# Rider products of two weight rows at a time in the expert passes of a hybrid encoder step

## The reference

```python
def _moe(h, w_router, b_router, we1, we3, we2):
    x = h.reshape(B * T, D)
    logits = (x @ w_router).astype(f32) + b_router.astype(f32)
    top_v, top_i = lax.top_k(logits, TOP_K)
    gates = jax.nn.softmax(top_v, axis=-1)
    comb = jnp.sum(jax.nn.one_hot(top_i, N_EXPERTS, dtype=f32) * gates[..., None], axis=1)
    y = jnp.zeros(x.shape, f32)
    for e in range(N_EXPERTS):
        y = y + comb[:, e:e + 1] * _swiglu(x, we1[e], we3[e], we2[e]).astype(f32)
```

## Time and profile before

| | |
|---|---|
| median of 3 runs | 2233.93 us (2231.75 to 2235.88) |
| the profiled execution | 2235.12 us |
| its span, first to last instruction | 2233.4 us |
| TensorE busy | 2063.2 us (92%) |
| VectorE busy | 1308.9 us (59%) |
| ScalarE busy | 996.8 us (45%) |
| mean granted TensorE clock | 0.935 of full speed |
| bytes moved by DMA | 418.23 MB, mean 187 GB/s |

### The profile page before, as it was taken

One profiled execution on the slowest core, in us unless ns is written; L12 is line 12 of the kernel. 1 busy time (PEld: TensorE's weight loads), 2 busy tenths in 40 slices (PEclk: granted clock), 3 DMA queues, 4 the chain that ended last, 5 costly groups with the idle time before them and its releaser, 6 DMA issues.

```text
span 2233.4 us, 36658 instructions
## 1 busy us (share of the span) xinstructions
PE 2063.2 (92%) x14266; PEld 1708.0 (76%) x14292; DVE 1308.9 (59%) x2052; ACT 996.8 (45%) x1456; POOL 181.5 (8%) x271
## 2 busy tenths in 40 slices
PE   6999878898999999998998788979899999999996
PEld 4999745588999999998997445966566657788883
DVE  2657654354544545456477553555565657789884
ACT  5522125444423443435211264435444556677772
POOL 3000120110000000000000111111010010000201
PEclk7999769999999999999997699978999999999998
DMA  9222668533545454642223357126677788899994
GB/s 328 65 76 76 162 189 292 183 122 95 167 126 165 136 157 132 172 126 78 61 73 85 89 190 239 47 93 236 202 262 233 242 271 311 327 372 373 375 382 179
DMA packets 272094, 418.23 MB, mean 187 GB/s; under 512 B 21214, under 2 KB 216312, under 8 KB 271952
## 3 DMA queue, kind: packets, MB, share of 16 engines
q1 hardware_dynamic: 249984, 349.50, 47.1%
q0 software_dynamic: 21968, 66.72, 9.2%
HBM read 385.73 MB, written 29.59 MB: 186 GB/s over the span
## 4 chain that ended last, share of the span: by engine, by line
PE 84%; DVE 5%; ACT 4%; DMA 3%; issue 2%; POOL 0%; ACTq 0%; PEldq 0%; DVEq 0%; PEld 0%; POOLq 0%; SPq 0%
PE banks L941 80%; PE banks L945 4%; DVE scratch L2522 1%; ACT scratch L1887 1%; DMA weight_ring<-in_w_ada 1%; DVE region L2522 1%; ACT hidden_t L1887 1%; ACT region_split L1887 1%; DMA scratch<-bias_rows 1%; ACT region L1887 0%; DVE weights_lower L2522 0%; DMA hidden_t<-h_rows,pass_tokens 0%; ACTq L1902 0%; DMA region<-in_pool_scale 0%; DMA expert_ring<-in_we 0%
## 5 line engine op out<-in xcount | busy, mean ns | idle before, releaser
L941 PE MATMUL banks<-upper_parts,region_split 128*128 128x320 f32 x1664 | 390.2, 310 | 4.5 <-DVE upper_parts L2522 4.5
L941 PE MATMUL banks<-upper_parts,weights_lower 128*128 128x320 f32 (+1 forms) x1248 | 387.1, 310 | 0.0
L2522 DVE TENSOR_TENSOR expert_lower<-expert_ring,region_split 128x1408 fp32r<-128x1408 f32 (+1 forms) x198 | 286.1, 1469 | 103.7 <-PE banks L941 78.3
L941 PE MATMUL banks<-region_split 128*128 128x320 f32 (+1 forms) x1264 | 342.1, 333 | 3.0 <-DVE upper_parts L2522 3.0
L941 PEld LDWEIGHTS banks<-upper_parts,region_split 128*128 128x128 f32 x1664 | 284.5, 189 | 4.8 <-issue 4.8
L1887 ACT ACTIVATE region_split<-expert_ring 128x1408 fp32r<-128x1408 f32 (+1 forms) x198 | 241.6, 1256 | 57.8 <-DMA expert_ring<-in_we 45.4
L941 PEld LDWEIGHTS banks<-region_split 128*128 128x128 f32 x1264 | 223.0, 188 | 25.0 <-issue 8.4
L941 PEld LDWEIGHTS banks<-upper_parts,weights_lower 128*128 128x128 f32 (+1 forms) x1248 | 235.3, 189 | 0.0
L941 PE MATMUL banks<-region_split,upper_parts 128*128 128x384 f32 x732 | 234.3, 385 | 0.0
L2522 DVE TENSOR_TENSOR weights_lower<-weight_ring,region_split 128x2048 fp32r<-128x2048 f32 (+2 forms) x72 | 168.9, 2350 | 96.2 <-ACT region_split L1887 96.2
L1887 ACT ACTIVATE region_split<-weight_ring 128x2048 fp32r<-128x2048 f32 (+2 forms) x72 | 140.6, 1958 | 164.2 <-PE banks L941 162.5
(11 more groups left out here) (333 smaller groups left out, 3276.1 us busy)
## 6 DMA issues: line engine op xcount, KB each, us to landing
expert_ring<-in_we SPq DMA_DIRECT2D x176, 704.0 KB, 6.3
expert_ring<-in_we SPq DMA_DIRECT2D x121, 512.0 KB, 4.3
weight_ring<-in_w_ada SPq DMA_DIRECT2D x48, 1024.0 KB, 9.3
weight_ring<-in_w SPq DMA_DIRECT2D x88, 512.0 KB, 4.8
weight_ring<-in_w_in SPq DMA_DIRECT2D x24, 1024.0 KB, 5.3
weight_ring<-in_w SPq DMA_DIRECT2D x16, 1408.0 KB, 6.2
weight_ring<-in_w_out SPq DMA_DIRECT2D x8, 1024.0 KB, 6.9
y_rows<-residual_t POOLq DMA_DIRECT2D x4, 1760.0 KB, 23.6
```

The lines of the kernel that those rows point to most:

```text
L941: return nc.tensor.matmul(out, lhsT, rhs, start=first, stop=last)
L2522: return v.tensor_tensor(out, x, y, op)
```

## The change

In `up` and `down` the ride behind each row's products becomes a pair of rides behind every other row's: in `up` behind the odd rows c (rows c + 5 and c + 6), in `down` behind the even rows f (f + 5 and f + 6). The two groups of rides ahead of the first `up`s have six rides where they had five. What each ride computes, the ring, the other engines' programs and the number of rides stay.

```diff
@@ up
                             release[0] = True
-                            if ridden and c + LOOK < UP_ROWS:
-                                ride(place - 1 + LOOK, up_row=c + LOOK)
-                            if following and c + LOOK >= UP_ROWS:
-                                ride(place - 1 + LOOK, down_row=c + LOOK - UP_ROWS)
+                            for ahead in range(c + LOOK, c + LOOK + 2) if c % 2 else ():
+                                if ridden and ahead < UP_ROWS:
+                                    ride(place - 1 + ahead - c, up_row=ahead)
+                                if following and UP_ROWS <= ahead < UP_ROWS + LOOK:
+                                    ride(place - 1 + ahead - c, down_row=ahead - UP_ROWS)
                             if c == 13:
                                 turn_rows(0, 0)
@@ down
                             release[0] = True
-                            if ridden and f + LOOK < NF:
-                                ride(place - 1 + LOOK, down_row=f + LOOK)
-                            if rows == "ridden" and f + LOOK >= NF:
-                                ride(place - 1 + LOOK, up_row=f + LOOK - NF)
+                            for ahead in range(f + LOOK, f + LOOK + 2) if f % 2 == 0 else ():
+                                if ridden and ahead < NF:
+                                    ride(place - 1 + ahead - f, down_row=ahead)
+                                if rows == "ridden" and ahead >= NF:
+                                    ride(place - 1 + ahead - f, up_row=ahead - NF)
                             if rows and f == 0:
@@ before the first two up
                     turn_riders(5)
-                    for c in range(LOOK):
+                    for c in range(LOOK + 1):
                         ride(c, up_row=c)
                     up(True, False)
                     turn_rows(1, 1)
                     turn_riders(3)
-                    for c in range(LOOK):
+                    for c in range(LOOK + 1):
                         ride(place + c, up_row=c)
```

## The result

The changed kernel took 2216.77 us (median of 6 runs, 2212.78 to 2223.65), the kernel before 2233.56 us beside it (6 runs, 2231.06 to 2235.88). The ratio is 0.9927, with a 95% interval of 0.9912 to 0.9942: 16.8 us less, which is more than the 0.2% that the prediction gave as what a measurement can tell. The forecast was 2214.0 in a range of 2210 to 2223.

What follows compares the result with a forecast made beforehand. TensorE, busy 92% of the span, was taken to bound the kernel. Savings of 14.3 + 5.0 + 1.3 + 0.6 = 21.2 us less 1.4 us of waits gave 19.8 off the 2233.93 us median: 2214 us, range 2210 to 2223.

Steps and rivals of the forecast that it cites:

- The switch: In `up` and `down`, 61 switches from products to rides and back go: 0.357 us behind up rows, 0.334 behind down rows.
- The turns at f = 9 and f = 1: In `down`, where a turn follows the ride: 0.22 us saved a switch, six switches, 1.3 us in all.
- The starting groups: Ahead of the first `up`s: second group's sixth ride hides in idle time, 0.64 us saved; first group's counts 0, at worst 0.64 more.
- The waits for landings: TensorE waits for weight rows ridden a step earlier: 0.4 us per loop trip (0 to 1.5), 0.2 behind the loop; 1.4 together.
- TensorE idle before rides with the ring as its releaser: Sign of being wrong: TensorE waiting before rides for expert ring rows would point to rivals A or C.
- The distance allowed: From a row's release to its ride as second of a pair: 8.1 us in `up`, 6.5 us in `down`.
- the need: Time from a row's release to its landing: 6.45 us for row 12, 6.75 us with the trip's slowest landing.
- one wait of 0.2 us: In the pass after the loop, row 17 has 0.1 us to spare before its ride; 0.2 us counted, from 0 to 1.
- nothing queued on VectorE or ScalarE waits longer: `claim`s, `lower`s and copies see each ride at the same step or earlier, so their queues gain no waiting.
- A: Rival: the gain is there but half is lost to landings in ridden passes, about 2225 us; chance 0.15.
- B: Rival: the cost comes with each ride, not the switch, so time stays within 0.2% of 2234 us; chance 0.05.
- C: Rival: slower, second rides wait for rows landing 8.5 us after release in `up`, 6.9 in `down`; about 2252 us; chance 0.03.

Runs made afterwards that it cites:

- late_pairs: Changed kernel with each pair asked a step later (first ride later, second at its old step), starting groups of five: 2215.32 us, ratio 0.9904 to the kernel before.
- double_apart: Kernel before with each ride's products done twice, the first half inside the row's products with a switch of its own: 2347.69 us.
- start_of_five: Changed kernel with five rides in the second starting group, the sixth again alone behind the first up row: 2220.50 us, one run.
- pairs_down_only: Kernel before with pairs of rides in `down` only; `up` and starting groups as before: 2227.12 us, one run.
- pairs_up_only: Changed kernel with single rides again in `down`, pairs in `up` and starting groups of six kept: 2222.85 us, ratio 0.9938 to the kernel before.
- pairs_again: The changed kernel run once more without edit: 2219.99 us against 2236.93 for the kernel before, ratio 0.9921.
- double_together: Kernel before with each ride's products done twice, back to back, no switch added: 2309.23 us, one run.
- triples: Changed kernel with groups of three rides behind every third row: 2213.93 us; with VectorE's token rows also moved ahead of row 18's lower part, 2205.50 us.

## Why the prediction was right, and where its sum was off

**The switch (20.6 of the 21.2 us).** Right in its price. 5.46 and 3.98 us for two rows with a pair, 69.90 us for a trip of late_pairs without waits where 69.8 to 70.0 was expected, and double_apart confirm a price that was only a difference of three rows. The first section fits too, -2.23 us for 6 switches (2.14), though 0.24 us of it is a cheaper sixth ride (below).

**The turns at f = 9 and f = 1.** Counted at 0.22 us a switch. By the rule that the prediction took from the Trainium skill (TensorEngine Tiling (Array Packing), Key Properties) the one at f = 9 would be worth 0.33. From the last product of the row to the first behind the turn the kernel before takes 1.41 us (1732.12 to 1733.53) with a ride of 0.643 in between, so 0.77 without it, and the changed one 0.48 (1719.39 to 1719.87). That is 0.29 us saved: nearer to the rule. At f = 1 the same reading gives 2.78 us before (1711.57 to 1714.35), 2.35 without its ride of 0.429, and 2.22 with the change (1698.93 to 1701.15): 0.13 us saved, less than was counted. Together the two come to 0.42 us a trip for the 0.44 in the sum, so the total was right by two errors that cancel.

**The starting groups.** The 0.64 us for the sixth ride of the second group stands (start_of_five). That of the first group lengthened the time to the first product by 0.40 us, from 6.07 to 6.47, less than a ride at the full clock, so the bound of 0.64 more was not drawn on. That time differs from one execution to the next, though: 5.75 to 6.07 us with five rides over the profiles of kernels that do each ride once, and 6.07 to 6.47 with six.

**The waits for landings: the term that was mis-sized.** Counted at 0.4 us a trip with an end at 1.5, and 0.2 once behind the loop. The trips gave back 0.9, 1.2 and 1.6 us (70.60, 70.92, 71.30 less 69.7), 3.6 us for the 1.2 counted. TensorE idle before rides with the ring as its releaser was one of the prediction's own signs of being wrong, and it is there. The place was right, row 12 at f = 6 of `down`; in the third trip row 11, whose ride keeps its step, was late as well (0.42 us), which the prediction had not priced. The distance allowed (6.5 us) was right as well; the need was not 6.45 us. Here are the first product of f = 4, which releases row 12's place, the two rides at f = 6, the second of them late, and the loads of rows 11 and 12, all in the changed kernel (issue, then issue to landing):

```profile
1705.23 0.39 PE L941 MATMUL banks<-region_split 128*128 128x512 f32 x1
...
1711.06 0.85 PE L941 MATMUL banks<-expert_ring,mix_t 128*32 128x384 f32 x8
1712.59 0.85 PE L941 MATMUL banks<-expert_ring,mix_t 128*32 128x384 f32 x8 [0.67 <-DMA expert_ring<-in_we]
...
L671 SPq DMA_DIRECT2D expert_ring<-in_we x1: 333/333/333, 1704.6 to 1704.6; - x1
DMA to landing us min/median/max: 6.2/6.2/6.2
...
L671 SPq DMA_DIRECT2D expert_ring<-in_we x1: 333/333/333, 1705.8 to 1705.8; - x1
DMA to landing us min/median/max: 6.8/6.8/6.8
```

Row 12 was released at 1705.23 and landed 7.4 us later, at 1712.6, where the earlier trace rows had made it 6.45. Before, the rows 11 and 12 were asked for 2.1 us apart; now they are 1.2 us apart, because two rows behind a pair of rides follow each other without a ride in between. In the three trips row 12 took 5.2, 5.8 and 5.2 us from issue to landing before, and 6.6, 6.8 and 7.2 with the change. The two half changes say where that comes from: 6.6 to 6.9 us in pairs_down_only, which has the close question and the old pace of `up`, and 5.2 to 5.8 in pairs_up_only, which has the faster `up` and the old spacing in `down`. The DMA engines are no fuller: over twelve microseconds around these loads their share is 0.85 before (from 1715) and 0.83 with the change (from 1703), and the same two gathers of GpSimd for the next pass land in that stretch in both. The issues are 1.2 us apart and the landings 1.8, so some 0.6 us is row 12 behind row 11. Row 11 itself took 6.0 to 6.7 us for 5.1 to 5.9. How the two loads share the engines was not tried, and that part stays argued. The prediction did say that "rows come closer together", but for the speed of the whole trip, and took the landing time from loads that were evenly spaced. A change that bunches the consumer bunches the releases too. The spacing should have been worked out like the distance was.

**What was not in the sum.** In the passes behind the loop one wait of 0.2 us had been counted. There were 0.49, 0.53 and 0.33 us for rows (the middle one is the row 17 that the prediction had named), and one of a kind that was not foreseen, 0.55 us for ScalarE. TensorE's timeline shows the wait, and ScalarE's two lines ahead of it the cause:

```profile
1859.65 0.50 PE L941 MATMUL banks<-z_weights_upper,upper_parts 128*128 128x512 f32 x1 [0.55 <-ACT hidden_t L1889]
...
1857.35 1.38 ACT L1889 ACTIVATE region_split<-expert_ring 128x1408 fp32r<-128x1408 f32 x1 [1.36 <-DMA expert_ring<-in_we]
...
1859.01 1.08 ACT L1889 ACTIVATE hidden_t<-banks 128x512 f32<-128x512 f32 x2
```

The rows came late for ScalarE as well. It stood 1.36 us for one, where the kernel before has 0.28 us at the same row, and its copies out of the banks, which TensorE's `claim` waits for, were queued behind it. The prediction said that nothing queued on VectorE or ScalarE waits longer, since no ride comes later; it had left out the landings themselves.

**The clock behind the second starting group** is where I put the 0.7 us of the second section. Two windows of the changed kernel, inside the six rides and over the first products:

```profile
1570.00:1571.00 1.00, 1.00 (x12) 0.38 (x8) 0.98 (x1) 0.00 (x0) 0.69 (x2) 0.50 0.78 327
...
1581.00:1582.00 1.00, 1.00 (x5) 1.00 (x4) 0.57 (x2) 0.96 (x2) 0.00 (x0) 0.50 0.07 16
```

In the kernel before the clock fell only in the idle time ahead of the first products and was back up with the first of them (0.91 from 1588 to 1589). In the changed kernel it fell to the 1.2 GHz level during the rides, rose, and fell again within the transposes and over the first row's products; these products took some 3.1 us for 2.1. The same section lost 0.9 to 1.0 us to its sum in pairs_again, late_pairs and start_of_five. It is not shown that the change brings this about. In pairs_down_only this section has the code of the kernel before, its clock stayed low until 1585.4 with products from 1582.2 on, and it took 56.82 us for 55.34. So the kernel before in its one profile may have been lucky by up to 1.5 us, and the 6.6 us given back are uncertain by as much. No kernel tested the clock by itself.

**The rivals.** A (half the gain lost, 2225) had the right mechanism at a third of its size: the trips gave back 3.6 us where it needed 12. B fell by double_together. C (slower) needed landings of 6.9 us after release in `down`, and 7.4 was reached for row 12. But its price was for three pairs of each `down` and seven of each `up`, and in the trips of `up` no ride waited. The condition came true for one row of a trip, and not at ten places.

**The total.** In the stretch 14.6 us for the 19.8 forecast; by the runs 16.8 us for 19.9 (2216.77 for 2214), the difference between two medians that each have their spread. The time lies inside the narrower 2211 to 2219 as well. The mechanism was right, and the term for the landings was a third of what it should have been; that the clock, ScalarE and the waits behind the loop added only some 3 us more is luck, for the sum had only 0.2 us for them.

**Left open.** The end of the expert stage, behind four plain passes, is the same code in all kernels, and took from 37.05 to 39.10 us (37.75 before, 37.05 in the changed kernel). What sets it wasn't tried, so the last line of the table is no gain of the change.

## What to carry to other kernels

Where small column-tiled products stand between full ones, read the price of going there and back from three rows (with, without, and in a run of their own), and group as many as the data's arrival allows: pairs gave 0.7 to 0.8% here, the late ones 1.0%, triples 1.4% once VectorE's order was mended. Group by delaying the first, not by asking earlier for the last: late_pairs had pairs with one wait left of seven. When a consumer is bunched, work out the new spacing of the releases and of the loads, and look down the in-order queues of the other engines for work that is ready but stands behind a bunched wait.

## What was not expected of the hardware

- A ride behind a ride costs its columns alone, 15.17 us for 27 rides where the columns say 15.0, while each switch there and back costs 0.31 to 0.36 us with 384 columns a tile, and 0.33 us with 256.
- TensorE's clock can fall while the engine is busy throughout. In double_apart it fell to the 1.2 GHz level for 3.4 us, behind 16 transposes of 32x32 and a row of products between small rides, in a trip without any idle time; in double_together, with the same transposes and the rides in one group, the clock stayed at 1.00 for the whole trip.
- Two loads of 704 KB issued 1.2 us apart took 6.2 and 6.8 us to land (6.6 to 7.2 for the second over the three trips), where the second took 5.2 to 5.8 us when issued 2.1 us behind the first.
